# Three weight slots throughout, reordered VectorE and ScalarE work at the heads and last rounds, and angle passes in two portions, in a float32 decoder trunk

## The reference

```python
def swiglu(h, wg, wu, wd):
    return (jax.nn.silu(h @ wg) * (h @ wu)) @ wd        # D_FF = 2816

for layer in range(2):
    h = rms_norm(x, ffn_norm[layer, 0])
    x = x + 0.5 * swiglu(h, ffn_w_gate[layer, 0], ffn_w_up[layer, 0], ffn_w_down[layer, 0])
    h = rms_norm(x, mix_norm[layer])
    if layer % 2 == 0:   # sparse attention over 8 heads beside a short convolution
        x = x + hybrid_mixer(h, positions, hyb_w_in[i], ..., hyb_w_out[i])
    else:                # causal means over 2, 4, 8, 16 tokens, then a product for each group
        x = x + pool_mixer(h, pool_w[i], pool_scale[i])
    h = rms_norm(x, ffn_norm[layer, 1])
    x = x + 0.5 * swiglu(h, ffn_w_gate[layer, 1], ffn_w_up[layer, 1], ffn_w_down[layer, 1])
```

## Time and profile before

| | us |
|---|---|
| median of 3 runs | 1709.23 (1706.83 to 1709.8) |
| the profiled execution | 1708.26 |
| its span, first to last instruction | 1706.2 |
| TensorE busy | 1680.2, 98% of the span |
| VectorE busy | 1298.6, 76% |
| ScalarE busy | 759.9, 45% |
| GpSimd busy | 119.9, 7% |

### The profile page before, as it was taken

One profiled execution on the slowest core, in us unless ns is written; L12 is line 12 of the kernel. 1 busy time (PEld: TensorE's weight loads), 2 busy tenths in 40 slices (PEclk: granted clock), 3 DMA queues, 4 the chain that ended last, 5 costly groups with the idle time before them and its releaser, 6 DMA issues.

```text
span 1706.2 us, 25926 instructions
## 1 busy us (share of the span) xinstructions
PE 1680.2 (98%) x10644; PEld 1494.8 (88%) x10644; DVE 1298.6 (76%) x1466; ACT 759.9 (45%) x1013; POOL 119.9 (7%) x115
## 2 busy tenths in 40 slices
PE   8899999999999999999999999999999899999998
PEld 6899999977876688999999889999998789999997
DVE  6987887766788659787887687877876888778774
ACT  7344435444337446434434464434434654444341
POOL 0600000032014220000000200000001000000000
PEclk9999999999999999999999999999999999999999
DMA  7242332253320034332421342422411344224221
GB/s 217 85 139 75 123 100 75 75 129 84 93 78 26 1 99 144 95 133 75 126 98 38 112 136 99 145 79 79 145 38 62 90 133 136 87 76 147 75 73 51
DMA packets 180922, 165.02 MB, mean 97 GB/s; under 512 B 15396, under 2 KB 156680, under 8 KB 180808
## 3 DMA queue, kind: packets, MB, share of 16 engines
q1 hardware_dynamic: 180232, 162.92, 30.6%
q10 hardware_dynamic: 576, 0.48, 0.1%
HBM read 160.89 MB, written 2.10 MB: 96 GB/s over the span
## 4 chain that ended last, share of the span: by engine, by line
PE 90%; DVE 5%; issue 3%; ACT 2%; DMA 0%; SPq 0%; POOL 0%; DVEq 0%; ACTq 0%
PE ps_s L750 19%; PE ps_s L752 19%; PE ps_s L751 19%; PE ps_y L750 5%; PE ps_y L751 5%; PE ps_y L752 5%; PE ps_stat L750 2%; PE ps_aux L750 2%; PE ps_aux L752 2%; PE ps_stat L752 2%; PE ps_aux L751 2%; PE ps_stat L751 2%; PE ps_s L1155 1%; PE ps_y L1184 1%; PE ps_aux L1204 1%
## 5 line engine op out<-in xcount | busy, mean ns | idle before, releaser
L750 PE MATMUL ps_s<-xg_hi,w_hi 128*128 128x256 f32 (+1 forms) x1280 | 410.7, 321 | 5.1 <-DVE work L1864 2.2
L751 PE MATMUL ps_s<-xg_lo,w_hi 128*128 128x256 f32 (+1 forms) x1280 | 407.3, 318 | 0.0
L752 PE MATMUL ps_s<-xg_hi,w_lo 128*128 128x256 f32 (+1 forms) x1280 | 407.3, 318 | 0.0
L1784 DVE TENSOR_TENSOR w_lo<-raw,w_hi 128x1024 fp32r<-128x1024 f32 (+2 forms) x210 | 254.6, 1213 | 156.6 <-ACT w_hi L1335 156.4
L750 PE MATMUL ps_s<-xt_hi,w_hi 128*128 128x256 f32 x1152 | 326.9, 284 | 3.4 <-ACT pair_gu L1335 2.9
L751 PE MATMUL ps_s<-xt_lo,w_hi 128*128 128x256 f32 x1152 | 326.8, 284 | 0.0
L752 PE MATMUL ps_s<-xt_hi,w_lo 128*128 128x256 f32 x1152 | 326.7, 284 | 0.0
L1335 ACT CAST w_hi<-raw 128x1024 fp32r<-128x1024 f32 (+1 forms) x212 | 217.8, 1028 | 196.0 <-PE ps_s L752 112.1
L750 PEld LDWEIGHTS ps_s<-xg_hi,w_hi 128*128 128x128 f32 x1280 | 244.4, 191 | 26.2 <-DVE xg_lo L1801 3.2
L751 PEld LDWEIGHTS ps_s<-xg_lo,w_hi 128*128 128x128 f32 x1280 | 244.3, 191 | 18.8 <-issue 1.4
L752 PEld LDWEIGHTS ps_s<-xg_hi,w_lo 128*128 128x128 f32 x1280 | 244.2, 191 | 16.7
(11 more groups left out here) (370 smaller groups left out, 2398.0 us busy)
## 6 DMA issues: line engine op xcount, KB each, us to landing
scratch<-in_ffn_w_down SPq DMA_DIRECT2D x64, 512.0 KB, 4.7
raw<-in_ffn_w_gate SPq DMA_DIRECT2D x48, 512.0 KB, 4.2
raw<-in_ffn_w_up SPq DMA_DIRECT2D x48, 512.0 KB, 6.1
raw_b<-in_ffn_w_gate SPq DMA_DIRECT2D x40, 512.0 KB, 5.0
raw_b<-in_ffn_w_up SPq DMA_DIRECT2D x40, 512.0 KB, 6.8
raw<-in_hyb_w_in SPq DMA_DIRECT2D x18, 512.0 KB, 3.8
raw<-in_ffn_w_down SPq DMA_DIRECT2D x8, 768.0 KB, 5.3
raw_b<-in_ffn_w_down SPq DMA_DIRECT2D x8, 768.0 KB, 5.3
```

Source lines behind the costliest of these rows:

```text
L750: mm(bank, hi, x_hi, start=first, stop=False, **kw)
L751: mm(bank, hi, x_lo, start=False, stop=False, **kw)
L752: return mm(bank, lo, x_hi, start=False, stop=last, **kw)
L1784: tt(shaped(weight(w_lo, n, 0, BLOCKS[n] * P)), source, shaped(f32(weight(w_hi, n, 0, BLOCKS[n] * P))), ALU.subtract).then_inc(lo_ready, 1)
```

## The change

1. `W_AT[n]` is now `n % 3 * WP` for all units, and a split waits for unit n-3 everywhere (`n - 2` as a count of units done). `W_FREE` is gone. Since the place of a unit now depends on its number, the loops over the first mixer's projections are written out three times on TensorE, ScalarE and VectorE. SyncE waits for the last unit of part 0 before it loads the gates' weights into memory that this part used.
2. Head 0: VectorE reads the reciprocal root and does `gate_of(0)`, `up_of(0)` and the split of unit 4 between its two `x_forms`.
3. Head 3: VectorE does `sums_low`, the reciprocal, `gate_of(0)` and `up_of(0)` ahead of both `x_forms`; ScalarE does `sums_high` ahead of its second `scale_x`, and `silu(0)` ahead of the copies of the differences. Heads 1 and 2 keep their order.
4. Last rounds: the split of unit d+3 comes behind `add_last(d)` on VectorE (before, the split of unit d+2 came ahead of it), and likewise on ScalarE; for the last unit no split is left.
5. The end of part 3: TensorE does `leave(6)` ahead of the second half of its last unit, VectorE does `leave(5)` and `leave(6)` ahead of `add_last(7)`, and the first half of the last tile is stored from ScalarE's queue.
6. The angle passes run in two portions of 8 and 9 instructions, behind the second and the fourth step of part 0.

```diff
-W_AT = [(n - U_MIX) % 2 * KH2 * P for n in range(U_END)]
-W_FREE = [n - 1 for n in range(U_END)]
+W_AT = [n % 3 * WP for n in range(U_END)]
...
-        W_AT[n] = j % 3 * WP
-        W_FREE[n] = n - (2 if j > 1 else 1)
...
+            sp.wait_ge(unit_done, U_MIX)
             sp.dma_start(gate_raw[:, :, :], blocks_of(w_in[:, COL_G:COL_G + 24])).then_inc(gate_w_landed, 16)
...
-            for h in range(2):
-                sp.wait_ge(end_copied[h], 1)
-                sp.dma_start(out[0, h * 2 * P:(h + 1) * 2 * P, D - P:D] ...
+            sp.wait_ge(end_copied[1], 1)
+            sp.dma_start(out[0, 2 * P:4 * P, D - P:D] ...
...  TensorE, last_round
                         leave(KD - 3)
+                        leave(KD - 2)
                         blocks(d, range(TAIL_TILES // 2, TAIL_TILES)).then_inc(unit_done, 1)
-                        leave(KD - 2)
                         leave_last()
...
-            with pe.Fori(1, 3) as i:
+            for i in (1, 2):
...  ScalarE
-                at_least(act, unit_done, W_FREE[n] + 4 * i)
+                n += 4 * i
+                at_least(act, unit_done, n - 2)
...  ScalarE, last_round
                 pair_of_silu(q_of(ffn, LAST))
+                split(u_last(ffn, 2))
+                pair_high(ffn, LAST)
                 for d in range(KD if ffn != 2 else KD - 2):
-                    if u_last(ffn, d) + 2 < U_END:
-                        split(u_last(ffn, d) + 2)
-                    if d == 0:
-                        pair_high(ffn, LAST)
+                    if d < KD - 1 and u_last(ffn, d) + 3 < U_END:
+                        split(u_last(ffn, d) + 3)
...  ScalarE, run_ffn (of version 5, head 3)
+                    scale_x(ffn, 0, R_FFN + KD * ffn)
+                    split(n + 3)
+                    if version == 5:
+                        sums_high(version)
+                        split(n + 4)
+                    scale_x(ffn, 1, R_FFN + KD * ffn)
                     root(f"x{version}", D)
                     nc.scalar.preload_act_table(ACT.Silu)
+                    split(n + (5 if version == 5 else 4))
...  ScalarE, the end
+            act.wait_ge(end_copied[0], 1)
+            act.dma_start(out[0, 0:2 * P, D - P:D] ...
...  VectorE, first_pairs
+                if version == 0:
+                    split(n + 2)
+                    first_rstd()
+                    split(n + 3)
+                    x_forms(ffn, 0)
+                    dve.wait_ge(stat_done, 1)
+                    nc.vector.tensor_copy(rstd[:, :], ps_stat[:, :]).then_inc(root_ready, 1)
+                    gate_of(0)
+                    up_of(0)
+                    split(n + 4)
+                    x_forms(ffn, 1)
+                    split(n + 5)
+                elif version == 5:
+                    sum_squares()
+                    split(n + 3)
+                    sums_low(version)
+                    split(n + 4)
+                    invert("x5", rstd[:, :])
+                    gate_of(0)
+                    up_of(0)
+                    x_forms(ffn, 0)
+                    split(n + 5)
+                    x_forms(ffn, 1)
...  VectorE, last_round
+                    if ffn == 3 and d == KD - 1:
+                        leave(KD - 3)
+                        leave(KD - 2)
                     add_last(ffn, d)
+                    if d < KD - 1 and n + 3 < U_END:
+                        split(n + 3)
                     if ffn < 3:
                         xg_low(version_out, d, gain)
...  GpSimd
-            pool.wait_ge(lo_ready, U_FFN[0] + 8)
-            for many in (1024.0, 1.0):
+            for many, steps_done in ((1024.0, 2), (1.0, 4)):
+                pool.wait_ge(turn_lo_ready, steps_done)
```

More of the change, by code:

```diff
@@ L1505, in run_ffn @@
                 n = U_FFN[ffn]
-                if version and version < 5:
-                    sums_high(version)
-                split(n + 2)
                 if version == 0:
+                    split(n + 2)
                     first_root()
@@ L1512, in run_ffn @@
                     split(n + 3)
-                for c in range(2):
-                    scale_x(ffn, c, R_FFN + KD * ffn)
-                    if version and c == (version == 5):
-                        split(n + 3)
-                if version == 5:
-                    sums_high(version)
-                if version:
+                    scale_x(ffn, 0, R_FFN)
+                    scale_x(ffn, 1, R_FFN)
+                    split(n + 4)
+                else:
+                    if version < 5:
+                        sums_high(version)
+                    split(n + 2)
+                    scale_x(ffn, 0, R_FFN + KD * ffn)
+                    split(n + 3)
+                    if version == 5:
+                        sums_high(version)
+                        split(n + 4)
+                    scale_x(ffn, 1, R_FFN + KD * ffn)
                     root(f"x{version}", D)
                     nc.scalar.preload_act_table(ACT.Silu)
+                    split(n + (5 if version == 5 else 4))
                 first_pairs(ffn)
@@ L1654, in convolved_high @@
                 copy(tile_of(ob_hi, j), at).then_inc(ob_hi_ready, 1)
-            with act.Fori(0, 3) as i:
+            for i in range(3):
                 project_four(0, i)
@@ L1878, in low_of @@
                     tt(tile_of(turn_lo, u), work[:, u % 2, :], f32(tile_of(turn_hi, u)), ALU.subtract).then_inc(act_lo_ready, 1)
-                split(n + 4)
-                gate_of(0)
-                up_of(0)
-                split(n + 5)
+                if version == 0:
+                    split(n + 2)
+                    first_rstd()
[12 more added lines that the diff above has]
+                    sums_low(version)
+                    split(n + 4)
+                    invert("x5", rstd[:, :])
+                    gate_of(0)
+                    up_of(0)
+                    x_forms(ffn, 0)
+                    split(n + 5)
+                    x_forms(ffn, 1)
+                else:
+                    sums_low(version)
+                    split(n + 2)
+                    x_forms(ffn, 0)
+                    split(n + 3)
+                    x_forms(ffn, 1)
+                    invert(f"x{version}", rstd[:, :])
+                    split(n + 4)
+                    gate_of(0)
+                    up_of(0)
+                    split(n + 5)
                 product_of(0)
@@ L2253, in convolved_low @@
                 tt(tile_of(ob_lo, j), at, f32(tile_of(ob_hi, j)), ALU.subtract).then_inc(ob_lo_ready, 1)
-            with dve.Fori(0, 3) as i:
+            for i in range(3):
                 project_four(0, i)
@@ L2386, in add_pooled @@
                     ALU.add).then_inc(x_ready, 1)
-            split(U_TAIL + 2)
             add_last(2, KD - 2)
+            split(U_GROUP[1])
             xg_low(4, KD - 2, R_MIX + KD)
-            split(U_GROUP[1])
             split(U_GROUP[2])
```

59 lines of the change are left out of this document (18 added, 41 removed).

## The result

Over four runs each, the changed kernel took 1690.51 us (1689.98 to 1691.23), the kernel before 1708.45 us (1706.83 to 1709.8). The ratio is 0.9896, with a 95% interval from 0.9879 to 0.9913. (The forecast was set against 1709.23, the median of the three runs known then; a fourth moved that median to 1708.45.) The profiled executions took 1690.82 and 1708.26 us, with spans of 1689.0 and 1706.2: 17.2 us of span.

What follows compares the result with a forecast made beforehand. TensorE, busy 98% of the span, was the bound: only its idle time (about 26 us) and low-clock stretches could be won. Terms for heads, last rounds, slots and end summed to 14.7 us: 1694.5 against 1709.23, range 1691 to 1700.

Steps and rivals of the forecast that it cites:

- Last rounds and slots: Waits behind parts 0 and 1 go, -1.5 and -1.2 us; with three slots the mixer's output-projection wait goes, -0.4.
- The end: End of part 3: last copy follows the transposes at once and SyncE has one store left, -1.3 us.
- The bounds: Limits on the gain at the end: 0.9 us if ScalarE's store is slow, 2.1 if stores land sooner alone.
- Head 0: Head 0 to the first step: 8.7 us of waits and low clock removed, 2.8 of new waits, net about -5.9.
- Head 3: Head 3: the wait at `total_stat` and low clock go, 6.7 us removed, 2.3 in new waits, net -4.4.
- Portions: Angle passes beside two steps of part 0: each costs VectorE 3 to 4 us, covered by slack, 0 net.
- the clock did not fall again: Rival: clock falls again in head 0 or head 3, giving 1696.2 to 1698.4 us; chance 0.17.
- the portions did not hinder: Rival: portions make VectorE late in two steps by up to 4 us each, 1696.5 to 1702.5; chance 0.13.
- VectorE's list did not stay at 70: Rival: VectorE alone sets head 0, m = 2 stays near 70 us, only 1 of 5.9 left, 1699.5; chance 0.08.
- no new wait stands in the projections: Rival: the mixer's written-out projections make TensorE wait for its instructions, 1712.8 us and more; chance 0.02.
- rival 4: Both heads: VectorE's hand-overs and the new waits shrink, 2 to 4 us more gain, 1690.5 to 1692.5; chance 0.12.

Runs made afterwards that it cites:

- e8: Changed kernel with two weight slots in the mixer and at each feed-forward part's first units, as before, loops still written out: 1693.07 us.
- e10: Changed kernel with two weight slots as before and the splits of the last rounds and part 2's end where they stood before: 1694.48 us.
- e5: Changed kernel with both stores of the last rows issued by SyncE, one after the other, as before: 1690.27 us.
- e6: Changed kernel with tile 6's transposes behind the last matmuls and the copies of tiles 5 and 6 behind `add_last(7)`, as before: 1692.70 us.
- e1: Changed kernel with GpSimd's 17 angle instructions run together in head 0, as before the change: 1697.73 us.
- e2: Kernel before the change with only the two portions of the angle passes added: 1702.63 us.
- e7: Changed kernel with VectorE's order in head 0 as before, angle passes still in portions: 1691.18 us.
- e3: Changed kernel with ScalarE's and VectorE's lists in head 3 as before: 1696.00 us.

## Why the prediction was wrong in size

The direction and each place were right; the sum was 14.7 where the spans show 17.2. No term was too large. Against the forecast of 1694.5 the result is 4.0 lower: 2.5 of it is the sum, 0.7 is what the medians show beyond the spans, and 0.8 lies in the 1709.23 that the forecast started from.

One price runs through all terms, and it was mis-sized. The prediction put a wait at its bracket and 0.1 to 0.15 us for filling the pipeline again. In the ledger each wait at the full clock costs 0.2 to 0.3 more than its bracket: 2.19 cost 2.48, 0.87 cost 1.10, 0.51 cost 0.76, 1.01 cost 1.28, 0.29 cost 0.56, 1.04 cost 1.31.

- **Last rounds and slots (3.1 forecast, 4.1 found) is the step that failed most.** In size: by places, 1.8 for 1.5 after part 0, 0.8 for 0.4 in the mixer, 1.3 for 1.2 after part 1, 0.15 for 0 at part 2's end. About 0.4 of the 1.0 is the price of the three waits, 0.1 the norm's matmuls, which cost 0.48 where 0.35 was taken, and 0.2 stands at places in the mixer without a bracket; the rest, part 2's end above all, I can't assign. In mechanism: the prediction had "TensorE had no wait in the projections, so there is nothing to win from the slots" and 0.4 for the mixer, and took the last rounds as a matter of order alone. e8 and e10 show that the slots carry part of the gain behind the last rounds, 2.9 us if undone, so the terms were also wrongly divided.
- **The end (1.3 forecast, 1.9 found).** Of the two edits, the prediction counted a store less on SyncE and took the copy's move as mostly paid for by later transposes. e5 and e6 show the reverse: the store is worth 0, the earlier `leave(6)` with its copies 2.0, through the stores that it takes out of the last one's way. The bounds, 0.9 to 2.1, held the number, but by luck: they were reasoned from the store.
- **Head 0 (5.9 forecast, 6.5 found).** The four old waits and the low clock were 9.0 in the ledger (8.7 forecast; the clock was 1.5 of it, where 1.7 was taken), and the waits that are there now cost 2.4 (2.8 forecast). The one at unit 6 was 0.82 for the 0.7 forecast. The wait at m = 2 was 1.06 for 2.1, since both its ends were off by 0.5: VectorE was there at 66.2, not 66.7 (GpSimd's hindrance was 4.1 and not 3.3), and TensorE came at 65.1, not 64.6. The prediction's list of parts was misleading in one respect: it counts 2.3 for the order. e1, e2 and e7 show at most 0.1 for the order and 6.4 for the portions.
- **Head 3 (4.4 forecast, 4.7 found).** Removed 6.7 as forecast; the new waits, 0.47 and 1.07, cost 2.0 with what is lost around them, where 2.3 was taken. e3 confirms both the wait and the clock's share.
- **Portions (0 forecast, 0 found).** Right, with more room than I gave it: 1.6 us of VectorE's time for both, where 3 to 4 each had been the estimate.

Of the rivals, the clock did not fall again, the portions did not hinder, VectorE's list did not stay at 70, and no new wait stands in the projections. What happened is rival 4 by its size, not by its mechanism: the new waits in both heads shrank by 0.7 us, not by 2 to 4. And 1690.51 lies in its 1690.5 to 1692.5 only at the very edge. The range was cut at 1691, inside that rival's own; taken in whole it would just have held the result.

## What to carry to other kernels

Waits in a chain of engines can't be added up as gains: follow the list of the engine that ends them, and ask what is at its end, not how long the bracket is. Here 2.5 us at unit 4 and 0.6 at unit 6 were worth 0, because VectorE's list decided at m = 2, while taking GpSimd's work away from that list was worth 6.4. And what an edit that frees a buffer is worth must be looked for wherever a split stands ahead of something urgent, not only where its own wait shows in the trace.
